# Hybrid decoder layer on one core: the state between two chunks replaced by an off-diagonal block of decays, head pairs taken two at a time

## What is computed

```python
Acum = jnp.cumsum(dt * A.reshape(G, R), axis=2)
seg = Acum[:, :, :, None] - Acum[:, :, None]
Lmat = jnp.exp(jnp.where(causal, seg, -jnp.inf))
CB = jnp.einsum('bclgn,bcsgn->bclsg', Cm, Bm)
Wm = CB[..., None] * Lmat * dt[:, :, None]
y_diag = jnp.einsum('bclsgr,bcsgrp->bclgrp', Wm, x)
decay_end = jnp.exp(Acum[:, :, -1:] - Acum)
chunk_states = jnp.einsum('bclgn,bclgr,bclgrp->bcgrpn', Bm, decay_end * dt, x)
y_off = jnp.einsum('bclgn,bcgrpn,bclgr->bclgrp', Cm, h_prev, jnp.exp(Acum))
y = y_diag + y_off
```

## Time and profile before

| | |
|---|---|
| median of 3 runs | 2837.32 us (2836.50 to 2838.19) |
| the profiled execution | 2837.04 us |
| its span, first to last instruction | 2835.3 us |
| TensorE busy, of the span | 99% |
| VectorE, ScalarE, GpSimd busy | 63%, 41%, 11% |
| DMA, mean over the span | 167 GB/s |
| mean granted TensorE clock | 0.998 |

### The profile page before, as it was taken

One profiled execution on the slowest core, in us unless ns is written; L12 is line 12 of the kernel. 1 busy time (PEld: TensorE's weight loads), 2 busy tenths in 40 slices (PEclk: granted clock), 3 DMA queues, 4 the chain that ended last, 5 costly groups with the idle time before them and its releaser, 6 DMA issues.

```text
span 2835.3 us, 53279 instructions
## 1 busy us (share of the span) xinstructions
PE 2804.5 (99%) x19312; PEld 2754.4 (97%) x19312; DVE 1781.2 (63%) x2250; ACT 1168.2 (41%) x1729; POOL 299.3 (11%) x456
## 2 busy tenths in 40 slices
PE   8899999999999999999999999999999999999998
PEld 7899999999999999999999999999999999999998
DVE  7888877887888655545455556555555555555564
ACT  5554453544544333333333335433333333333553
POOL 2222221212222100000000001000000000000100
PEclk9999999999999999999999999999999999999999
DMA  7787887787878665555555554555555555555463
GB/s 200 207 211 185 208 223 182 196 213 194 210 185 207 179 176 149 152 146 149 152 151 141 149 150 144 159 149 148 148 148 151 150 145 151 149 150 154 134 181 112
DMA packets 893378, 474.15 MB, mean 167 GB/s; under 512 B 154089, under 2 KB 886689, under 8 KB 892977
## 3 DMA queue, kind: packets, MB, share of 16 engines
q1 hardware_dynamic: 819097, 431.02, 56.2%
q10 hardware_dynamic: 73528, 39.39, 4.8%
q0 software_dynamic: 672, 2.66, 0.2%
HBM read 447.50 MB, written 25.47 MB: 167 GB/s over the span
## 4 chain that ended last, share of the span: by engine, by line
PE 96%; DVE 1%; SPq 1%; DMA 1%; ACT 0%; issue 0%; ACTq 0%; DVEq 0%
PE ps L1715 30%; PE ps L1716 30%; PE ps L1717 30%; PE ps L2104 1%; SPq L598 1%; PE ps L1863 1%; PE ps L1958 1%; PE ps L1821 1%; PE ps L1864 1%; PE ps L2117 0%; PE ps L1873 0%; PE ps L1975 0%; PE ps L2074 0%; DMA raw<-in_w_in 0%; PE ps L2088 0%
## 5 line engine op out<-in xcount | busy, mean ns | idle before, releaser
L1715 PE MATMUL ps<-n_hi,whi 128*128 128x320 f32 x4144 | 1287.2, 311 | 2.6 <-DVE wlo L1086 2.0
L1717 PE MATMUL ps<-n_hi,wlo 128*128 128x320 f32 x4144 | 1282.2, 309 | 0.0
L1716 PE MATMUL ps<-n_lo,whi 128*128 128x320 f32 x4144 | 1282.1, 309 | 0.0
L1086 DVE TENSOR_TENSOR wlo<-raw,whi 128x1024 fp32r<-128x1024 f32 x746 | 921.5, 1245 | 466.6 <-ACT whi L719 465.5
L719 ACT ACTIVATE whi<-raw 128x1024 fp32r<-128x1024 f32 x746 | 784.8, 1057 | 831.8 <-PE ps L1717 742.7
L1715 PEld LDWEIGHTS ps<-n_hi,whi 128*128 128x128 f32 x4144 | 778.8, 188 | 6.2 <-DVE wlo L1086 2.8
L1716 PEld LDWEIGHTS ps<-n_lo,whi 128*128 128x128 f32 x4144 | 778.8, 188 | 1.4
L1717 PEld LDWEIGHTS ps<-n_hi,wlo 128*128 128x128 f32 x4144 | 778.5, 188 | 0.0
L1715 PE MATMUL ps<-c_hi,whi 128*128 128x320 f32 x1728 | 535.9, 310 | 0.5 <-DVE c_lo L1200 0.5
L1717 PE MATMUL ps<-c_hi,wlo 128*128 128x320 f32 x1728 | 534.5, 309 | 0.0
L1716 PE MATMUL ps<-c_lo,whi 128*128 128x320 f32 x1728 | 534.4, 309 | 0.0
(11 more groups left out here) (299 smaller groups left out, 1774.2 us busy)
## 6 DMA issues: line engine op xcount, KB each, us to landing
raw<-in_w_in SPq DMA_DIRECT2D x322, 512.0 KB, 4.6
raw<-in_w_ffn_gate SPq DMA_DIRECT2D x88, 512.0 KB, 4.5
raw<-in_w_ffn_up SPq DMA_DIRECT2D x88, 512.0 KB, 5.0
raw<-in_w_ffn_down SPq DMA_DIRECT2D x88, 512.0 KB, 4.3
raw<-in_w_ssm_out SPq DMA_DIRECT2D x64, 512.0 KB, 6.2
hq<-in_state_ssm SPq DMA_DIRECT2D x512, 32.0 KB, 3.0
hs<-in_state_ssm ACTq DMA_DIRECT2D x32, 512.0 KB, 5.2
out_ssm_sample<-hs ACTq DMA_DIRECT2D x32, 512.0 KB, 3.4
```

Source lines behind the costliest of these rows:

```text
L1086: tt(wlo[slot][:], raw[slot][:], whi[slot][:].bitcast(F32), SUB).then_inc(lo_split, 1)
L1715: mm(out, w_h, x_h, start=first, stop=False)
L1716: mm(out, w_h, x_l, start=False, stop=False)
L1717: return mm(out, w_l, x_h, start=False, stop=last)
```

## The change

The first chunk's state is no longer made for the second chunk's output. Instead the decays between a token of chunk 0 and one of chunk 1 are treated as one more block of `wm` (quads 5 and 6). SP loads exp(Acum) of chunk 1 for the group's eight heads into all partitions (`load_off`, 512 KB), `bc` gets one more product (C of chunk 1 with B of chunk 0), which VectorE copies to `cb_off`, and GpSimd multiplies it in (two products of 128x512 in `clamp`). The in-chunk products add that block, with `xwe` of chunk 0, to the second chunk's in the same bank. `ssd3`, L2117 and the copy to `h1t` are gone. `last` makes chunk 0's state by four products in place of four turns. The sample chunk's products take all 128 rows, of which VectorE clears the upper 64 once, in group 0. The old state's turned output now lies in the same bank as the pair's sum. TensorE takes pairs 0 and 1 together in the step `pair` 0, and pairs 2 and 3 in the step `pair` 2: first the in-chunk products of both, then both turns, then the four carry products. The banks and waits are changed to fit. `ea` keeps 73 of the 200 columns. `gcol` moves to an unused part of `cbm`.

```diff
...
         head = (x(1) + [("dtend", 0)] + x(2) + [("flip", 0)] + x(3) + [("dtab", 0)] + x(4)
...
-                ("ssd3", 0), ("pair", 0), ("flip", 1)]
+                ("pair", 0), ("flip", 1)]
...
         head = (x(0, 1) + [("norm", 0)] + x(2) + [("lows", 0)] + x(3) + [("bc", 0)] + x(4)
...
-        tail = [("unit", "z", 0), ("ssd1", 0), ("unit", "z", 1), ("flip", 1), ("ssd3", 0), ("pair", 0)]
+        tail = [("unit", "z", 0), ("ssd1", 0), ("unit", "z", 1), ("flip", 1), ("pair", 0)]
...
-        wm = s1("wm", [P, 5, 512])
-        ea = s1("ea", [P, 4, P + NS + NB])
-        h1t = s1("h1t", [P, 512])
+        cb_off = s1("cb_off", [P, P])
+        wm = s1("wm", [P, 7, 512])
+        ea = s1("ea", [P, 4, 1 + NS + NB])
...
-        yoffs = s1("yoffs", [P, P + NS])
+        yoffs = s1("yoffs", [P, NS])
...
-        gcol = s1("gcol", [P, K_X + 1, 6])
+        gcol = cbm[:, 2, NS:NS + 6 * (K_X + 1)].rearrange("p (k t) -> p k t", t=6)
...
-        HN_BANKS, LAST_BANKS = ((7, 2), (7, 2), (4, 5), (7, 2)), (4, 5)
-        YOFF_BANKS, YD_BANKS, OLD_BANKS = (3, 3, 1, 3), (6, 6, 0, 6), (3, 5)
+        HN_BANKS, LAST_BANKS = ((7, 2), (4, 5), (4, 5), (7, 2)), (7, 2)
+        Y_BANKS, OLD_BANKS = (6, 3, 6, 3), (3, 6)
+        OFF_COLS, OLD_COLS = slice(NT, NT + P), slice(NT, NT + P)
...
-        N_CONSTS, DVE_LINKS = 8, {"ssm": 36, "sc": 8, "mix": 4, "ffn": 8, "ple": 4}
+        N_CONSTS, DVE_LINKS = 8, {"ssm": 32, "sc": 8, "mix": 4, "ffn": 8, "ple": 4}
...
-        h1_done, h1_kept, hfin_stored = sem("h1_done"), sem("h1_kept"), sem("hfin_stored")
+        hfin_stored, off_loaded, off_weighed = sem("hfin_stored"), sem("off_loaded"), sem("off_weighed")
...
                 for half in range(2):
...
-                                 of_half[:, at(4 * g, 4)].broadcast_to([HD, 4, P + NS + NB])
+                                 of_half[:, at(4 * g, 4), P - 1:P + NS + NB].broadcast_to([HD, 4, 1 + NS + NB])
                                  ).then_inc(ea_loaded, 16)
+            def load_off(g):
+                wait(sp, yd_done, 4 * g)
+                sp.dma_start(wm[:, 5:7, :].rearrange("p q (h n) -> p (q h) n", n=P),
+                             decays[:, at(g, 1, HPG), 0:P].broadcast_to([P, HPG, P])).then_inc(off_loaded, 16)
...
             def visit(seg, it):
...
-                        for place, part in zip((12, 12, 12, 14) if seg.start == 0 else (12, 13, 14, 16), range(4)):
+                        for place, part in zip((12, 12, 12, 13, 14) if seg.start == 0 else (12, 13, 14, 15, 16), range(5)):
...
-                                load_sums(it, part) if part < 3 else load_decays(it)
+                                load_sums(it, part) if part < 3 else load_off(it) if part == 3 else load_decays(it)
...
                     for half in range(2):
...
-                elif kind == "ssd3":
-                    act.wait_ge(h1_done, g + 1)
-                    activate(h1t[:], ps[:, 2, :], copy).then_inc(h1_kept, 1)
                 elif kind == "old":
...
-                                        scale=ea[:, q, P - 1:P])
+                                        scale=ea[:, q, 0:1])
...
                 elif kind == "pair":
                     if j == 2:
...
             def own_columns(bank):
...
-                return (ps[:, bank, 2 * P:3 * P].rearrange("p (b w) -> p b w", b=4)[:, :, 0:2 * LB]
+                return (ps[:, bank, OLD_COLS].rearrange("p (b w) -> p b w", b=4)[:, :, 0:2 * LB]
...
             def add_ple(it, j):
...
             def close_pair(g, j):
...
                 y = chunk[:, j, :]
-                dve.wait_ge(yoff_done, 4 * g + j + 1)
-                own(tt(yoffs[:, 0:P], ps[:, YOFF_BANKS[j], 0:P], ea[:, j, 0:P], MUL))
-                own(tt(yoffs[:, P:P + NS].rearrange("p (h b l) -> p b h l", h=2, l=LB), own_columns(YOFF_BANKS[j]),
-                       ea[:, j, P:P + NS].rearrange("p (h b l) -> p b h l", h=2, l=LB), MUL))
-                own(tt(y[:, P:NT], y[:, P:NT], yoffs[:], ADD))
+                own(tt(yoffs[:].rearrange("p (h b l) -> p b h l", h=2, l=LB), own_columns(Y_BANKS[j]),
+                       ea[:, j, 1:1 + NS].rearrange("p (h b l) -> p b h l", h=2, l=LB), MUL))
+                own(tt(y[:, SEQ:NT], y[:, SEQ:NT], yoffs[:], ADD))
...
             def dt_parts():
...
+                    v.memset(xdt[NS:P, 2, :], 0.0)
+                    dve.wait_ge(row_sums, 1)
+                    v.memset(wm[NS:P, 4, :], 0.0)
                 elif kind == "unit" and step[1] == "c":
...
+                    v.tensor_copy(cb_off[:], ps[:, 6, OFF_COLS])
...
                 elif kind == "pair":
                     y = chunk[:, j, :]
...
+                    dve.wait_ge(yoff_done, 4 * g + j + 1)
...
-                    own(stt(y, xs[:, j, :], gd[:, j:j + 1], ps[:, YD_BANKS[j], 0:NT], MUL, ADD))
+                    own(stt(y, xs[:, j, :], gd[:, j:j + 1], ps[:, Y_BANKS[j], 0:NT], MUL, ADD))
                     for half in range(2):
...
+                elif kind == "clamp":
+                    pool.wait_ge(off_loaded, 16 * (g + 1))
+                    pool.wait_ge(cbm_ready, g + 1)
+                    for quad in (5, 6):
+                        w3 = wm[:, quad, :].rearrange("p (h n) -> p h n", n=P)
+                        g_.tensor_tensor(w3, w3, cb_off[:].unsqueeze(1).broadcast_to([P, 4, P]), ALU.mult
+                                         ).then_inc(off_weighed, 1)
                 elif kind == "pair":
...
                     for half in range(2):
...
-                                         ea[:, j, P + NS + 4 * half:P + NS + 4 * half + 4].unsqueeze(2)
+                                         ea[:, j, 1 + NS + 4 * half:1 + NS + 4 * half + 4].unsqueeze(2)
...
                 if kind == "x":
...
-                    if j == 0:
-                        wait(pe, hn_added, 8 * g - 3)
-                    elif j == 1:
-                        wait(pe, yg_ready, 4 * g - 1)
+                    if j < 2:
+                        wait(pe, z_ready, 4 * g - 1 + j)
...
-                        pe.wait_ge(hn_added, 8 * GROUPS - 3)
...
             def old_output(g, r):
...
-                if r == 0:
-                    wait(pe, yg_ready, 4 * g)
-                else:
-                    wait(pe, out_added, 8 * g)
+                wait(pe, yg_ready, 4 * g + r)
                 for half in range(2):
...
+            def in_chunk(g, j):
+                if j == 2:
+                    pe.wait_ge(yo_kept, 2 * g + 2)
+                if j == 3:
+                    pe.wait_ge(yg_ready, 4 * g + 2)
+                bank = Y_BANKS[j]
+                for c, of, first, last in ((0, 0, True, True), (1, 2, True, False), (1, 5, False, True), (2, 4, True, True)):
+                    rows = P if c < 2 else NS
+                    x = xwe[:, 0, :] if of == 5 else xdt[:, c, :]
+                    for i in range(2):
+                        h = 2 * j + i
+                        quad_i = of + h // 4 if c < 2 else of
+                        m = h % 4 if c < 2 else h
+                        end = mm(ps[i * HD:(i + 1) * HD, bank, token_rows(c)], x[:, h * HD:(h + 1) * HD],
+                                 wm[:, quad_i, m * rows:(m + 1) * rows], start=first, stop=last)
+                end.then_inc(yd_done, 1)
+            def turn_old(g, j):
+                pe.wait_ge(yo_kept, 2 * g + j // 2 + 1)
+                turn(ps[:, Y_BANKS[j], OLD_COLS], yo[:, j * P:(j + 1) * P], ident[:]).then_inc(yoff_done, 1)
             def carry_in(g, j):
...
-                if j == 2:
+                if j == 3:
...
                 for half in range(2):
-                    if j % 2:
-                        pe.wait_ge(hn_added, 8 * g + 2 * (j // 2) + half + 1)
+                    if j == 2:
+                        pe.wait_ge(hn_added, 8 * g + 2 + half + 1)
...
+                        if c == 1:
+                            mm(ps[:, 6, OFF_COLS], bc[:, 0, token_rows(0)], bc[:, 1, token_rows(1)], start=True, stop=True)
...
                 elif kind == "ssd1":
...
-                elif kind == "ssd3":
-                    pe.wait_ge(xw_ready, 2 * g + 2)
-                    pe.wait_ge(b_stacked, 2 * g + 2)
-                    mm(ps[:, 2, :], bt[:, 0, :], xwe[:, 0, :], start=True, stop=True).then_inc(h1_done, 1)
                 elif kind == "old":
...
                 elif kind == "last":
-                    pe.wait_ge(yo_kept, 2 * g + 2)
+                    pe.wait_ge(hn_added, 8 * g + 2)
...
-                        last = turn(ps[:, LAST_BANKS[0], q * P:(q + 1) * P], h1t[:, q * P:(q + 1) * P], ident[:])
+                        last = mm(ps[:, LAST_BANKS[0], q * P:(q + 1) * P], xwe[:, 0, q * P:(q + 1) * P], bt[:, 0, :],
+                                  start=True, stop=True)
                     last.then_inc(last_done, 1)
...
                     last.then_inc(last_done, 1)
                 elif kind == "pair":
-                    pe.wait_ge(w_ready, 5 * g + 5)
-                    pe.wait_ge(cbm_ready, g + 1)
```

(41 more changed lines are left out.)

## The result

The changed kernel took 2842.71 us (2839.86 to 2849.88, 14 runs) where the kernel of before took 2837.3 beside it: ratio 1.0021, 95% interval 1.0014 to 1.0028. It is slower by 5.4 us; 7.5 us faster was forecast. Its times also spread over 10 us, those of before over 3. The profiled execution took 2841.72 us, span 2839.9.

The account below looks back on a forecast made before the run. TensorE, busy 99% of the span, was taken as the bound. Seven groups at 1.0 us (7.0), 0.3 in group 0 and 0.2 for its carry products gave 7.5: 2837.3 to 2829.8 us, range 2828.0 to 2833.2.

Parts of the forecast that it names:

- 1.0 us a group: TensorE's blocks in groups 1 to 7: 10.56 us become 9.58, taken as 1.0 gained, seven times: 7.0.
- the padded sample chunk: In-chunk products: contracting over 128 rows, 64 of them zero, turns the 0.21 step into 0.11 per record pair.
- Rivals 2 and 3: Sample chunk's padding: saves nothing, gain 4.3, 2833.0 us, chance 0.08; or costs 7.0 us, 2836.8, chance 0.03.
- The Trainium skill's rule on small dimensions: Sample chunk: dimensions of 64 or less can gain up to a factor of two; padding would then cost 7.0 us.
- the paragraph on what is hidden: Work on ScalarE, VectorE, GpSimd and DMA queues: all claimed covered by slack, costing TensorE nothing.
- 18 us of cover for 2.2: GpSimd's two products, 1.10 us each, start at 530.3; GpSimd's next wait is at 551.17, so they cost nothing.
- those pieces are three (10 us) ahead of TensorE: SP's queue: the new load stands before the next weight pieces, which have 10 us in hand, so it costs nothing.
- Rival 5: At b_stack: GpSimd's products hold VectorE their whole 2.2 us; 2.9 a group, 20.3 less 7.5, 2850 us; chance 0.05.
- `out` 0, L1821, the pair block: Places in groups 1 to 7 where any wait of TensorE would show the forecast wrong.
- that rule: VectorE and GpSimd share an SBUF port pair under exclusive lock; VectorE could lose up to what GpSimd adds.
- 0.5 us of gain: Group 0: 0.3 from TensorE's blocks around the wait for masks, 0.2 from carry products no longer awaiting stacked x.
- after it restarts the same masks, clock and DMAs stand as before: Group 0 behind the masks' wait, ending at 110.35: the 1.2 GHz stretch stays, with 0.3 to 0.5 us either way.

Follow-up runs that it names:

- e8: e6 with the sample chunk contracting over its 64 rows again instead of 128: 2840.03 us (1.0002 to 1.0021 of the kernel of before).
- e1: The changed kernel with GpSimd's two products cut from 1024 columns to 8 each, load kept: 2831.53 us (0.9970 to 0.9989).
- e2: The changed kernel with the off-diagonal decays' load cut to one partition, GpSimd's products kept: 2830.99 us (0.9964 to 0.9985).
- e3: The changed kernel with both GpSimd's products cut to 8 columns and the load cut to one partition: 2828.80 us (0.9962 to 0.9982).
- e6_again: The kernel of e6 run once more, unchanged: 2830.30 us (0.9966 to 0.9986).
- e7: The changed kernel, but in groups 1 to 7 GpSimd does its products after the last output's add: 2833.04 us (0.9976 to 0.9995).
- e6: The changed kernel with the load's source packed and, in groups 1 to 7, the two products on VectorE: 2830.24 us (0.9967 to 0.9985).

## Why the prediction was wrong

**TensorE's work: right in direction, undersized.** Forecast 1.0 us a group, measured 1.37 (113.38 to 112.01). The mis-sized term is the padded sample chunk. I took 0.11 for a record pair over 128 rows with 64 columns, since no row showed that form; it costs 0.055. With that, the new two-pair block is 2.99 instead of 3.19, twice a group, which is 0.4: the whole difference. Rivals 2 and 3 (the padding saves nothing, or costs) fall by e8: it saves 7 us of the kernel's time, and without it half a microsecond a group would be left (113.38 to 112.88). The Trainium skill's rule on small dimensions (TensorEngine Tiling (Array Packing), section Theoretical Speedup), weighed in the prediction, would have it the other way round; nothing in these runs shows a cheap form over 64 rows.

**The step that failed is the paragraph on what is hidden, where GpSimd's two products and their load are priced at nothing.** Three things in it went wrong together.

- "the next thing GpSimd has to wait for is at 551.17: 18 us of cover for 2.2". That is GpSimd's own queue, and there it was true: the two products took 2.55 us, and its next wait ends at 551.71. But what they held up was VectorE, which was by then splitting the piece in front of an output's add. One paragraph on I wrote that the new instructions "will stretch VectorE too" and named no instruction that they would fall on.
- "those pieces are three (10 us) ahead of TensorE". So they were, but the load that I said would take about as long as wm<-acum, 5.6 us, took 10.1, and the piece behind it came late enough that ScalarE waited 1.77 us for it.
- Each was judged alone against its cover. e1 and e2 show that in the six groups each is in fact fully covered (112.01 us a group, as in e3). The sum isn't: it costs 10.0 us in the six waits, 2.6 before group 1 and 7.4 behind it.

**Rival 5 had the mechanism and the wrong place.** It forecast 2850 by GpSimd's products holding VectorE at b_stack. There was no stall at b_stack, and none of the pair blocks waited in groups 1 to 7. The place was some 20 us behind b_stack in the same group (510.69 and 533.16 in the change), at the outputs' adds, a part of VectorE's queue that I had not looked at because TensorE waits for nothing there in the kernel of before. It is also at none of the places where I had said that a wait would prove me wrong: `out` 0, L1821, the pair block. A slack that no wait shows is there all the same, and the change spent 3.5 us of 2.4.

**The port.** While GpSimd's L1650 ran, VectorE's split stood, and then GpSimd's copy stood for VectorE (0.21 to 1.21). By the Trainium skill, SBUF — State Buffer, section "SBUF: two separate sides", one of the two has the port pair for its whole instruction and the other blocks. The trace agrees: the split began while L1643 still ran (to 528.69), and its 3.92 is about the time to the end of GpSimd's products (531.21 - 528.37 = 2.84) and one undisturbed split (1.22). I had cited that rule in the prediction, and let it change no term of the sum. The trace shows more than one blocked instruction, too: the split had stood since 528.37, and neither the end of L1643 (528.69) nor that of the first product (529.92) let it in, only that of the second. In the kernel of before it was let in at the first such end:

```profile
528.24 2.02 POOL L1636 TENSOR_TENSOR wm<-wm,hcol 64x512 f32<-64x512 f32 x1
```

There the split, begun at 527.20, ended 1.12 us behind the start of this last subtraction, which took 2.02 us where it takes 1.04 in the change. What decides who is let in isn't shown; a split can lose a whole run of GpSimd's instructions, not only one.

**Group 0: partly open.** I forecast 0.5 us of gain. Compared at `ssd1` of group 1, the change lost 2.4, and e3 gained 1.3. The loss is the longest of the six waits for an add, among the outputs of group 0, which TensorE makes ahead of that `ssd1`; VectorE's split beside GpSimd's products, and TensorE:

```profile
190.08 3.93 DVE L1090 TENSOR_TENSOR wlo<-raw,whi 128x1024 fp32r<-128x1024 f32 x1 [3.54 <-ACT whi L726]
...
194.87 0.41 PE L1729 MATMUL ps<-c_hi,whi 128*128 128x320 f32 x1 [2.37 <-DVE acc_a L1419]
```

From the first in-chunk product of group 0 to `ssd1` of group 1 the change takes 106.3 us, and e3, e6_again and e7, which have no such wait, 103.7. So it costs 2.6 us, and without it the change would have come to that `ssd1` 0.2 us ahead of the kernel of before. What happened up to that product nearly cancels out. The chain in the change is: the sums land later, GpSimd's subtractions start at 89.33 instead of 88.47, ScalarE's last silu ends late, and TensorE waits 4.6 us for it:

```profile
99.04 2.82 PE L2107 MATMUL ps<-ident,xs 128*128 128x128 f32 x12 [4.60 <-ACT xs L885]
113.16 0.66 PE L1973 MATMUL ps<-wm,xdt 128*64 128x128 f32 x8 [3.06 <-issue]
...
100.00:110.00 10.00, 10.00 (x57) 9.69 (x55) 6.16 (x9) 7.88 (x11) 0.00 (x0) 0.78 0.83 171
110.00:116.00 6.00, 2.94 (x38) 2.49 (x38) 5.69 (x10) 0.44 (x1) 0.60 (x1) 1.00 1.10 247
```

The last two rows are windows (length, busy time of TensorE, its loads, VectorE, ScalarE and GpSimd, then the granted clock). The granted clock was between its two levels, 1.2 and 2.4 GHz, behind the first wait (0.78 over 100 to 110) and full behind the second, the other way round than in the earlier trace rows, so the masks' end moved from 110.35 to about 113. The 2.8 us are given back behind it: the kernel of before, at the lower clock and with the old blocks, takes 106.7 us from its first in-chunk product to `ssd1` of group 1. I had argued that "after it restarts the same masks, clock and DMAs stand as before". They don't: the same wait for ScalarE is 4.7 us in e3 too, so it needs neither the load nor the products. And in two profiles of one kernel (e6, e6_again) `ssd1` of group 1 differs by 2.1 us. Why the sums land later in the changed kernels wasn't settled.

**Behind the groups** the 3.0 us are a wait at the start of the next segment and what follows it. Timeline of TensorE, and a window of the same kernel:

```profile
951.60 0.63 PE L1729 MATMUL ps<-n_hi,whi 128*128 128x320 f32 x1 [2.86 <-DVE wlo L1090]
...
950.00:960.00 10.00, 8.40 (x38) 8.40 (x39) 8.28 (x14) 4.27 (x5) 3.78 (x3) 0.66 0.60 197
```

The wait was 1.0 us before, and the granted clock of that window was 1.00; here the engine stood for 2.86 and got 0.66. In e1 the longest such wait is 1.3, the clock stays at 1.00 and the stretch behind the groups takes 1935.5 us; in the change it takes 1939.7. The other runs, with 1.3 to 2.5 us of it, lie between (1935.9 to 1939.2). Ahead of that split in the change stands ScalarE, which waited 6.36 us, until 944.6, for stores of out_ssm_sample to land (4.04, until 942.5, before). That the changed kernels' wider spread comes from here and from group 0 is likely, but wasn't tested.

## What to carry to other kernels

Price an instruction given to GpSimd by what VectorE does beside it, and follow VectorE's queue from there to the next semaphore for which TensorE waits, even where the profile shows no wait: an absent wait has a slack, and it must be read off the timeline before it is spent. Add up all new delays in front of the same semaphore, DMA and engine alike; two that alone cost nothing in the six groups cost 7.4 us there together, and 13.9 us in the whole kernel where either alone costs under 3. And a load is priced by its rows and its neighbours, not by its kilobytes.

## What was not expected of the hardware

- In the paired fp32 products over 128 rows, 64 columns start 0.055 us apart and 128 columns 0.11. Over 64 rows, 64 columns take 0.11, with 0.21 on the way down and 0.155 back. Zero-padding the short contraction saved 0.22 us per head pair.
- Two loads of 512 KB on the same queue to the same tile landed after 5.4 us (rows of 4 KB) and 10.1 (512 bytes); in 4-KB rows at the second's place it was 8.3.
- A GpSimd copy of 0.21 us took 1.21 while VectorE split beside it: the hold goes both ways. A split that had stood since 528.37 was passed over at 528.69 and 529.92 and let in at 531.2, at the end of a run of GpSimd's instructions.
